# Dilated attention: first steps moved into the value groups, and the index keys' group splits its next weight slab first

## The reference, cut to what matters

```python
# first block, layer 1: three groups of heads, (window, dilation) = (128, 1), (512, 4), (2048, 16)
qkv = einsum('bsd,de->bse', h, w_qkv); q = rope(q) * hd ** -0.5; k = rope(k)
s = where(mask, q @ k.T, NEG_INF); m = max(s); e = exp(s - m); o = (e / sum(e)) @ v
merged = concat(o_g * 3 * softmax(lse over the groups)_g) @ w_out
# second block, each layer: token_mix
p = h @ w_in                        # u, va, q, k, v, index queries iq, index keys ik, index weights
score = sum_h w_h * relu(iq_h @ ik) # per query, its 128 best keys are kept for the attention
```

## Time and profile before

| | |
|---|---|
| median of three runs | 3000.38 us (2998.42 to 3000.57) |
| the profiled execution's own time | 2999.97 us |
| its span, first to last instruction | 2998.2 us |
| PE busy | 2948.5 us, 98% of the span |

### The profile page before, as it was taken

The page is one execution under the profiler, slowest core; times in us unless marked ns, Lnnn a source line. Parts: engine busy times, 40 slices in busy tenths (PEclk is TensorE's granted clock), DMA queues, the critical chain, the costliest instruction groups (busy, mean ns, idle before and its releaser), DMA issues.

```text
span 2998.2 us, 47467 instructions
## 1 busy us (share of the span) xinstructions
PE 2948.5 (98%) x18016; PEld 2608.7 (87%) x18016; DVE 2238.7 (75%) x3253; ACT 1318.8 (44%) x1975; POOL 189.1 (6%) x267
## 2 busy tenths in 40 slices
PE   8999999999999999999999999999999999999998
PEld 7888888787999889998787899988998878799987
DVE  7577766655877788877688787778777678788753
ACT  4432323465555345442345555425454244654442
POOL 0000001200000000000130000000000023000000
PEclk9999999999999999999999999999999999999999
DMA  4366564411333633345332133462335432133332
GB/s 159 100 195 192 180 210 138 132 44 57 99 105 109 216 125 99 102 143 172 94 91 64 57 106 105 147 217 87 108 107 182 122 105 85 43 92 100 103 106 77
DMA packets 268334, 357.77 MB, mean 119 GB/s; under 512 B 19907, under 2 KB 211765, under 8 KB 268177
## 3 DMA queue, kind: packets, MB, share of 16 engines
q1 hardware_dynamic: 241344, 270.57, 28.8%
q0 software_dynamic: 26352, 84.74, 8.8%
q10 hardware_dynamic: 480, 0.29, 0.0%
HBM read 348.69 MB, written 2.10 MB: 117 GB/s over the span
## 4 chain that ended last, share of the span: by engine, by line
PE 85%; DVE 9%; ACT 2%; issue 2%; DMA 1%; POOL 0%; DVEq 0%; SPq 0%; ACTq 0%
PE bank L2313 16%; PE bank L2315 15%; PE bank L2314 15%; PE bank L2459 11%; PE bank L2461 11%; PE bank L2462 11%; DVE w_lo L1371 1%; ACT w_hi L780 1%; PE bank L2336 1%; PE bank L2337 1%; PE bank L2339 1%; DVE h_f L1427 1%; PE bank L2374 1%; DMA swap<-st 1%; DVE h_lo L1433 1%
## 5 line engine op out<-in xcount | busy, mean ns | idle before, releaser
L780 ACT ACTIVATE w_hi<-raw 128x1024 fp32r<-128x1024 f32 x308 | 325.8, 1058 | 749.0 <-PE bank L2315 706.0
L1371 DVE TENSOR_TENSOR w_lo<-raw,w_hi 128x1024 fp32r<-128x1024 f32 x288 | 351.9, 1222 | 369.0 <-ACT w_hi L780 366.2
L2313 PE MATMUL bank<-act_hi,w_hi 128*128 128x512 f32 (+1 forms) x1120 | 438.7, 392 | 0.0
L2315 PE MATMUL bank<-act_hi,w_lo 128*128 128x512 f32 (+1 forms) x1120 | 436.4, 390 | 0.0
L2314 PE MATMUL bank<-act_lo,w_hi 128*128 128x512 f32 (+1 forms) x1120 | 435.9, 389 | 0.0
L2313 PE MATMUL bank<-h_hi,w_hi 128*128 128x512 f32 x1056 | 417.5, 395 | 6.7 <-DVE w_lo L1371 6.1
L2314 PE MATMUL bank<-h_lo,w_hi 128*128 128x512 f32 x1056 | 412.7, 391 | 0.0
L2315 PE MATMUL bank<-h_hi,w_lo 128*128 128x512 f32 x1056 | 412.6, 391 | 0.0
L2459 PE MATMUL bank<-s_tile,w_hi_more 128*128 128x256 f32 x1200 | 339.8, 283 | 0.3
L2462 PE MATMUL bank<-s_tile,w_lo_more 128*128 128x256 f32 x1200 | 339.6, 283 | 0.0
L2461 PE MATMUL bank<-s_tile,w_hi_more 128*128 128x256 f32 x1200 | 339.6, 283 | 0.0
(11 more groups left out here) (383 smaller groups left out, 6282.7 us busy)
## 6 DMA issues: line engine op xcount, KB each, us to landing
raw<-in_ffn_w_in_dram SPq DMA_DIRECT2D x176, 512.0 KB, 3.5
ada_w<-in_ada_w_dram POOLq DMA_DIRECT2D x72, 1024.0 KB, 5.6
raw<-in_ffn_w_out_dram SPq DMA_DIRECT2D x88, 512.0 KB, 3.6
raw<-in_ffn_w_gate_dram SPq DMA_DIRECT2D x44, 512.0 KB, 3.8
raw<-in_ffn_w_up_dram SPq DMA_DIRECT2D x44, 512.0 KB, 3.8
raw<-in_ffn_w_down_dram SPq DMA_DIRECT2D x44, 512.0 KB, 4.1
raw<-in_mix_w_in_dram SPq DMA_DIRECT2D x44, 512.0 KB, 3.7
raw<-in_attn_w_qkv_dram SPq DMA_DIRECT2D x24, 512.0 KB, 3.6
```

The costliest lines, as they stand in the source:

```text
L780: nc.scalar.activation(w_hi[:, nb % SPL, :], raw_slab(nb), ACT.Copy).then_inc(s_hi, 1)
L1371: V.tensor_tensor(w_lo[:, nb % SPL, :], raw_slab(nb), w_hi[:, nb % SPL, :].bitcast(F32), ALU.subtract).then_inc(s_lo, 1)
L2313: T.matmul(dst, wh, mh, start=first, stop=False)
L2315: return T.matmul(dst, wl, mh, start=False, stop=last)
```

## The change

It has two parts.

**Dilated attention.** PE makes the scores of steps 0 and 1 behind group 9 and those of steps 2 and 3 between the halves of group 11; those of steps 4 and 5 follow the last value transposes. DVE masks steps 0 and 1 amid `scaled_values` of tiles 0 and 1, steps 2 and 3 at slot 23 (second half of group 11); in the loop, steps 4 and 5 at steps 0 and 1, and from step 3 on again step s + 3. ACT takes the exponentials of steps 0 and 1 at slot 21 (second half of group 10) ahead of that slot's split; the load of the exponential's table moves from slot 23 to slot 19. The ring of banks begins with 6 and 7. `st_v` gets a place of its own, because `P` lies where it was. The six `keep_warm` matmuls of step 0 go.

**Index keys' group.** In a group of one slab (group 1 of m = 1 and 2) ACT and DVE split slab n+2 first, before they rotate, round or copy anything.

```diff
+        a1["st_v"] = place("a1_st_v", [P, 2, S], at=sq_at)
-        STEP_BANKS = (0, 1, 6, 7)
+        STEP_BANKS = (6, 7, 0, 1)
+        EARLY_STEPS = 2
@@ ACT, project
+                        if slabs == 1:
+                            split_hi(n + 2)
                         if j == 0 and turned:
                             rotated_hi(*turned[0])
...
-                        if slot < 23:
+                        if m == 0 and slot == 21:
+                            for s in range(EARLY_STEPS):
+                                step_exps(s)
+                        if slot < 23 and slabs == 2:
                             split_hi(n + 2 + j)
-                        elif m == 0:
+                        if m == 0 and slot == 19:
                             nc.scalar.activation(scratch1[:], small[:, 65:66], ACT.Exp)
@@ ACT, dilated_attention (step_exps holds the lines taken out here)
-                act.wait_ge(s_postmm, 8)
...
+                    if s >= EARLY_STEPS:
+                        step_exps(s)
@@ DVE, project
-                        scaled_values(tiles, 2 if tiles[-1][1] == V_EARLY - 1 else 0)
+                        scaled_values(tiles, EARLY_STEPS if tiles[0][1] == 0 else 0)
...
+                        if slabs == 1:
+                            split_lo(n + 2)
                         if j == 0:
                             rotate(turned[0:1])
...
-                        if slot < 23 if m == 0 else n + 2 + j - nb < POOL_LO[0]:
+                        if slabs == 2 and (slot < 23 if m == 0 else n + 2 + j - nb < POOL_LO[0]):
                             split_lo(n + 2 + j)
...
+                        if m == 0 and slot == 23:
+                            mask_step(2)
+                            mask_step(3)
...
-                else:
-                    mask_step(2)
@@ DVE, dilated_attention
-                    if s + 3 < n_steps:
+                    if s < 2:
+                        mask_step(s + 4)
+                    elif 5 < s + 3 < n_steps:
                         mask_step(s + 3)
@@ PE, project
+                            if m == 0 and g == 11 and half == 0:
+                                pe.wait_ge(s_actT, at + counts[10])
+                                step_scores(2)
...
+                    if m == 0 and g == 9:
+                        pe.wait_ge(s_post, 16)
+                        step_scores(0)
...
-                if m == 0:
-                    pe.wait_ge(s_actT, AT0["out0"] - 2)
-                    step_scores(0)
-                    step_scores(2)
...
                 posts(pending)
+                if m == 0:
+                    step_scores(4)
@@ PE, dilated_attention
-                    keep_warm({0: 6, 2: 6, 3: 4, 6: 6, 7: 6, 9: 6, 11: 6}.get(s, 0), 2 + s % 2)
+                    keep_warm({2: 6, 3: 4, 6: 6, 7: 6, 9: 6, 11: 6}.get(s, 0), 2 + s % 2)
...
-                    if s % 2 and s + 3 < n_steps:
+                    if s % 2 and 4 < s + 3 < n_steps:
                         step_scores(s + 3)
```

More of the change, by code:

```diff
@@ L1200, in mix, with step_exps @@
                 scaled_hi(NB - 1)
+            def step_exps(s):
+                act.wait_ge(s_masked, s + 1)
+                if s >= 2:
+                    act.wait_ge(s_tr, s - 1)
+                for u, _, _, off, n, _ in A0[s][2]:
+                    ins = nc.scalar.activation(a1["P"][:, s % 2, off:off + n], bank[STEP_BANKS[s % 4]][:, off:off + n], ACT.Exp,
+                                               scale=-1.0, bias=sum_col(0, u), accum_out=sum_col(1, u))
+                ins.then_inc(s_exp, 1)
             def dilated_attention():
                 nh, b_, n_steps = 16, a1, len(A0)
-                act.wait_ge(s_postmm, 8)
                 def split_v(c):
```

## The result

| | before | after |
|---|---|---|
| median of the runs timed together | 2997.99 us (22 runs) | 3002.36 us (22 runs) |
| ratio, 95% interval | | 1.0015, 1.0009 to 1.0021 |
| span of the profiled execution | 2998.2 us | 3000.5 us |
| PE busy in it | | 98%, mean granted clock 0.993 |

The change costs 4.4 us (2.7 to 6.3 by the interval), 0.15%: slower, by less than the 0.2% that I had called no change. The prediction's +3.6 us (+3.2 on the median) is close to that. Its 3003.6 was counted from one execution of 2999.97 us; timed again beside the changed kernel, the kernel before has 2997.99 in place of the 3000.38 of three runs. The parts of that sum are not all as close, and this is what the rest is about.

A forecast was written before the change was run, and what follows sets the result against it. PE, busy 98% of the span, was taken to bound the kernel. Terms -0.3 + 0.6 - 1.2 + 1.05 + 2.4 + 1.05 = +3.6 us on 2999.97 gave 3003.6; own range 3001 to 3006, overall 2998.9 to 3006.9.

The forecast's parts named there:

- dilated, step 0's low part: Start of dilated attention: DVE begins step 0's low part at 633.1 in place of 633.41, -0.3 us; bounds -1.5 and +0.7.
- dilated, clock: Start of dilated attention: slower PE clock after a new 1.9 us of idle PE, +0.6 us.
- m = 1, wait moved: Index keys' group, m = 1: 2.39 us wait goes, most of it moves to group 3, -1.2 us; bounds -2.4 and 0.
- m = 2, wait: Ahead of group 3, m = 2: PE waits +2.4 us more for slab nb+5; bounds +1.9 and +3.7.
- (1): Sign at m = 1: no wait for slab nb+4, a wait of about 3 us for nb+5.
- (2): Sign at m = 2: first iq rotation near 3.8 us later against ik slab's end, PE's 0.66 us grown to about 3.
- (3): Sign: granted clock under 1.00 behind either wait, at m = 1 and m = 2.
- (5): Sign in dilated attention: step 0's low part within 1 us of its old distance from group 11's end, less 1.6.
- (4): Sign in the value groups: scores amid groups 9 and 11 bring no new wait of PE.
- The rival by which the words of the change come true: m = 1 wait and slow 1.6 us go without new wait, dilated attention wins 1.5: 2994.5 us, chance 0.08.
- the one by which m = 2 stays as before: Index keys' group, m = 2: split of nb+4 comes late anyway, chain as before: 2998.5 us, chance 0.07.
- The rival of the clock: Three new idle PE stretches, first dilated attention's start, make it slower by clock: 3007.5 or 3011 us, chance 0.15.

The follow-up runs named there:

- The work on constants: Index keys' part alone on the kernel before, plus 18 matmuls on constants in front of group 3: 2998.14 against 2997.87 us, ratio 1.0001.
- the m = 1 edit alone: Early split of slab nb+4 at m = 1 only, on the kernel before: 2997.90 us, ratio 0.9996 (0.9986 to 1.0005).
- nb+5, then the relus: Kernel before with splits of nb+4 and nb+5 first: 2995.79 us; also first two heads' relus ahead of second query tile's rounding: 2994.48 us.

## Why the prediction was right, and where its steps were not

The mechanism was the one foreseen: the wait moves to slab nb+5, and m = 2, which had nearly none, gets one. The terms:

| step | predicted, us | the runs show, us |
|---|---|---|
| dilated, step 0's low part | -0.3 | +0.5 |
| dilated, clock | +0.6 | 0 |
| m = 1, wait moved | -1.2 | -1.06 (group 3's first matmul: 1490.10 to 1486.93, less 2.11) |
| m = 1, clock behind it | +1.05 | +1.6 |
| m = 2, wait | +2.4 | +2.39 (3.05 - 0.66) |
| m = 2, clock behind it | +1.05 | +1.5 (+1.43 at group 3's first matmul to +2.96) |
| sum | +3.6 | +4.9; displacements of the three places +4.8; medians +4.4 |

Both clock terms of the last column are what the stretch behind group 3's start cost in this pair of traces. At m = 1 the kernel before paid the like ahead of group 3, behind its wait for nb+4; the two rows for m = 1 together (+0.54) are no more than its traces differ by among themselves.

**The chain behind the split** held in its length. From ACT's split of nb+4 to DVE's low part of nb+5 I had 12.85 us at m = 1 (1474.65 to 1487.5) and 12.8 at m = 2 (2419.3 to 2432.1); the trace has 12.95 and 12.80. PE's wait at m = 2 came out to 0.01 us. I had it run through the landing of ik's swap; the rows do not show that this was its last link. In the trace after, the low part of the second iq tile ends at 2427.29 (2426.60 + 0.69) and the rotation of ik starts at 2427.40, with no wait for the swap put down to it, so DVE's own order and the landing come out too close to tell apart. What is queued behind a waiting split on an engine that works in program order was the whole of it; the Trainium skill ("PSUM — Partial Sum Buffer", section "Engine vs sequencer instructions") calls the queues of ScalarE, VectorE and GpSimdE strictly first in, first out, and the trace agrees: the iq tile's rotation, ready in time before, started 2.24 us behind the start of the split.

**The clock** was the mis-sized term. I gave each stall ahead of group 3 two thirds of 1.6 us, and 0.6 to the stall in dilated attention. The work on constants shows 1.56 and 1.50 for the two, and dilated attention paid nothing. Of the eight waits of 2.39 to 3.3 us in these groups, over six profiles, every one has a stretch at half the clock that begins at its end or already within it. The contrary row, 1.08 us at 585.63, and the new 1.74 have none, and are shorter than all eight. The rule weighed in the prediction, the Trainium skill's "TensorE: Matmul & The Clock Gate", section "HAM oscillation", tells of a kernel in which PE waits about 3 to 5 us for each burst and begins it cold; taken for these stalls it puts the full 1.6 on both and the sum at 4.7. The traces agree with it at all eight waits, and two of these, 2.39 and 2.6 us, are shorter than those of its example.

**The dilated part** erred in sign. The scores of steps 0 to 3 took 1.6 us in one run between transposes; amid the groups they cost 2.27: the transposes of tiles 4 and 5 are at 629.07 in place of 626.00, less the 0.80 by which this trace ran late before the value groups. The tail of the value tiles, which I named as what is late next, starts 0.67 us later than I had it, and so step 0's low part comes 0.52 us late (634.73 less 633.41 less 0.80), where I had -0.3. It stayed within the bound of +0.7. That DVE's queue sets it is shown by the kernel with the mask of step 4 taken out from ahead of it: there it starts 0.15 us behind the scaling of tiles 6 and 7. That dilated attention's total, +0.3 predicted and +0.5 measured, came so close is luck: the clock's +0.6 stood in for the late tail.

**What would show it**: points (1), (2), (3) and (5) are in the rows above; (4) holds, since in the value groups PE has no new wait (the 1.08 us at 585.63 are 1.11); the 0.39 us at 630.58 lie behind them, ahead of the last transposes. The rival by which the words of the change come true fell with the m = 1 edit alone; the one by which m = 2 stays as before, with its 3.05. The rival of the clock got two of its three half-clock stretches, and the third place, the start of dilated attention, on which it rested first of all, not. One slip there: the first rival's own sum is 5.5 us, short of the 0.2% (6 us), so "a good half of it past the 0.2%" does not follow from it; nothing else rests on that.

**What stays open**: a half-clock stretch near 653 us, in the middle of dilated attention, is in 4 of the 10 profiles of this study, 3 of them with dilated attention as before and 1 with it changed; why it comes in one execution and not in another was not tried. Stretches near 740 and 1450 us are in all ten, with no idle time of PE over 1.4 us around them, so a single long wait is not the only thing that such a stretch follows. Why the wait for nb+4 at m = 1 is 2.39, 2.6 or 3.3 us with one and the same order was not looked into. Nor was a kernel tried that splits nb+5 first and keeps the order of before for nb+4 at m = 2, where the early split has nothing to win.

## What to carry to other kernels

When work is moved ahead of a wait on an engine that runs in program order, list what then stands behind that wait, in each layer that shares the code: the same edit was worth nothing that can be told at m = 1 and cost 3.8 us at m = 2, since only there had the queue behind it been on time. Look for the reorder that leaves the late item itself first (nb+5, then the relus), not the one that frees its neighbour. And price a stall of a busy PE with the clock behind it: here 3 us of waiting cost 4.6.

## What the runs showed of the hardware

Eighteen matmuls on constants in front of a late slab, 2.41 us of work that computes nothing, took 3.1 us (by displacement) off the kernel over two layers, without the slab coming any sooner (0.71 and 0.62 us of waiting left). With the early split at m = 1 alone the granted clock fell already while PE still waited 3.3 us, and 12 matmuls ran at 0.50 in place of 9 behind the 3.20 us of after; waits of nearly one length therefore do not always have the same price.
